# Expert slots that belong to one row tile of tokens, with scatter products on 64 partitions each

## What is computed

```python
def hier_moe(t, w_route_group, w_route_expert, w_gate_up, w_down):
    g_logits = jnp.einsum('td,dg->tg', t, w_route_group, ...)
    grp = jnp.argmax(g_logits, axis=-1)
    ...
    top_v, top_i = lax.top_k(e_prob, 2)
    ...
    for g in range(N_EXPERT_GROUPS):
        gu = jnp.einsum('td,edf->tef', t, w_gate_up[g])
        act = silu(gu[..., :512]) * gu[..., 512:] * combine[:, g, :, None]
        out = out + jnp.einsum('tef,efd->td', act, w_down[g])
    return out
```

## Time and profile before

| | us |
|---|---|
| median of 3 runs | 1650.46 (1649.89 to 1651.84) |
| the profiled execution | 1652.1 |
| its span | 1650.3 |
| TensorE busy in the span | 1601.2 (97%) |
| VectorE, ScalarE busy | 619.9, 449.0 |
| granted TensorE clock, mean | 0.994 |
| first expert layer's products | from 309 to 774 |
| second expert layer's products | from 1178 to 1642 |

### The profile page before, as it was taken

How to read it: one execution, slowest core, us unless ns; L and a number is a source line. 1 busy time by engine, 2 the same in 40 slices (tenths; PEclk the granted TensorE clock), 3 DMA queues, 4 the chain that set the end, 5 groups by cost and what they waited for, 6 DMA issues and landing times.

```text
span 1650.3 us, 21196 instructions
## 1 busy us (share of the span) xinstructions
PE 1601.2 (97%) x7929; PEld 934.2 (57%) x7929; DVE 619.9 (38%) x1356; ACT 449.0 (27%) x1168; POOL 142.2 (9%) x295
## 2 busy tenths in 40 slices
PE   9998879999999999999999999999999999999997
PEld 7877667653444344344877888877653444344342
DVE  4589993321322222123023544554421322222123
ACT  3488872211111111112143142232311111111112
POOL 1233341100000000001001202230000000000000
PEclk9999989999999999999999999999999999999999
DMA  9668777499999999999434956696599999999995
GB/s 340 204 212 264 219 237 286 151 400 401 427 428 424 429 428 424 430 425 399 175 132 162 331 183 239 173 275 285 226 401 402 429 426 425 429 427 426 430 424 214
DMA packets 107589, 542.24 MB, mean 329 GB/s; under 512 B 8780, under 2 KB 33556, under 8 KB 78546
## 3 DMA queue, kind: packets, MB, share of 16 engines
q1 hardware_dynamic: 90518, 485.20, 73.0%
q0 software_dynamic: 16672, 55.53, 10.7%
q10 hardware_dynamic: 316, 0.37, 0.1%
HBM read 524.81 MB, written 16.45 MB: 328 GB/s over the span
## 4 chain that ended last, share of the span: by engine, by line
PE 78%; DVE 10%; DMA 5%; ACT 4%; issue 2%; POOL 0%; SPq 0%; DVEq 0%; ACTq 0%
PE bank L1049 25%; PE bank L1413 14%; PE bank L1061 13%; PE bank L1032 5%; PE bank L1055 4%; PE bank L884 4%; DMA ring<-in_moe_w_gate_up 3%; PE bank L1344 3%; PE bank L1316 3%; DVE arena L2452 2%; PE bank L1642 2%; DVE arena L2297 2%; PE bank L1075 1%; ACT arena L1764 1%; DVE arena L2460 1%
## 5 line engine op out<-in xcount | busy, mean ns | idle before, releaser
L1049 PE MATMUL bank<-ring,arena 128*64 128x512 f32 x1520 | 335.7, 592 | 2.9 <-DMA ring<-in_moe_w_gate_up 2.8
L1413 PE MATMUL bank<-hT,ring 128*128 128x264 f32 x1152 | 269.4, 389 | 0.2
L1413 PEld LDWEIGHTS bank<-hT,ring 128*128 128x128 f32 x1152 | 214.4, 190 | 41.2 <-issue 3.9
L1049 PEld LDWEIGHTS bank<-ring,arena 128*64 128x64 f32 x1520 | 111.7, 137 | 214.4 <-issue 214.1
L2297 DVE TENSOR_TENSOR arena<-arena,bank 128x512 f32<-128x512 f32 x32 | 34.2, 1070 | 389.2 <-ACT arena L1764 389.2
L1061 PE MATMUL bank<-ring,arena 128*64 128x512 f32 x768 | 170.1, 595 | 1.6 <-DVE arena L2218 1.6
L1055 PE MATMUL bank<-arena 128*128 128x512 f32 x256 | 127.0, 618 | 1.6 <-ACT arena L1774 1.6
L1764 ACT ACTIVATE arena<-bank 128x512 f32<-128x512 f32 x32 | 19.1, 597 | 386.0 <-PE bank L1049 386.0
L2244 DVE SCALAR_TENSOR_TENSOR arena<-arena 128x1024 f32<-128x1024 f32 x32 | 41.1, 1284 | 213.2 <-ACT arena L1774 213.2
L1049 PE MATMUL bank<-arena 128*64 128x512 f32 x512 | 112.6, 592 | 0.0
L1061 PEld LDWEIGHTS bank<-ring,arena 128*64 128x64 f32 x768 | 53.8, 137 | 101.8 <-issue 99.7
(11 more groups left out here) (348 smaller groups left out, 1713.2 us busy)
## 6 DMA issues: line engine op xcount, KB each, us to landing
ring<-in_moe_w_gate_up SPq DMA_DIRECT2D x78, 2048.0 KB, 18.6
ring<-in_moe_w_down SPq DMA_DIRECT2D x48, 2048.0 KB, 23.6
arena<-in_moe_w_gate_up SPq DMA_DIRECT2D x32, 2048.0 KB, 18.9
ring<-in_attn_qkv SPq DMA_DIRECT2D x18, 2048.0 KB, 11.6
ring<-in_moe_w_gate_up SPq DMA_DIRECT2D x34, 1024.0 KB, 17.6
arena<-in_moe_w_down SPq DMA_DIRECT2D x32, 1024.0 KB, 21.2
ring<-in_ssm_in_proj SPq DMA_DIRECT2D x10, 2048.0 KB, 14.2
out<-arena POOLq DMA_DIRECT2D x24, 512.0 KB, 4.3
```

The source lines that it names most:

```text
L1049: mm = pe.matmul(bank[j][e * SLOTS:(e + 1) * SLOTS, :], Xg[:, 4 * half + k, 2 * (p % 2) + e, :], gate_rows(2 * half + e, p, k, first)[:, j ...
L1413: mm = pe.matmul(bank[i % 2][:, 0:T], wv[:, k, (i % 4) * P:(i % 4 + 1) * P], hT[:, k, :], start=(n == 0), stop=(n == DT - 1))
```

## The change

Slots now belong to a tile: each expert has 2 x 32 slots, 28 for prompt tokens of that tile and 4 for sample tokens (HALF = 32, FREE = 28, SAMP = 4; still 5 possible rounds). Ranks are counted per tile, so the product across tiles goes. A gather writes each tile's columns without adding up: 112 columns instead of 224. The gate, up and down products and the weight stream stay as they are. ScalarE copies the result rows in four pieces of 32 partitions per half, so that rows lie tile by tile (tile 0 on partitions 0 to 63, tile 1 on 64 to 127). A scatter then uses its tile's 64 partitions, and the first two scatters of a pair are of the two tiles, same half of the width. The shares are transposed by matmuls against the identity onto those partitions, and `CmT` is half as wide. Gathers 0 and 1 are moved up, ahead of the wait for the product. After the last pair the scatters go tile by tile.

```diff
-FREE = SLOTS - NS
-ROUNDS = -(-TP // FREE)
+TILES = TP // P
+SAMP = NS // TILES
+FREE = SLOTS // TILES - SAMP
+ROUNDS = -(-P // FREE)
+HALF = SLOTS // TILES
...
-                for t in range(2):
-                    for u in range(t + 1):
-                        mm = pe.matmul(bank[0][:, (t + 1) * NE:(t + 2) * NE], (strict if u == t else ones)[:, :], msk[:, u, :],
-                                       start=(u == 0), stop=(u == t))
-                mm.then_inc(m_rk, 1)
+                pe.matmul(bank[0][:, NE:3 * NE], strict[:, :], msk[:, 0:2, :].rearrange("p t e -> p (t e)"),
+                          start=True, stop=True).then_inc(m_rk, 1)
...
+                    out = bank[4 + i % 2][:, 0:16 * FREE].rearrange("p (d e t s) -> p d e t s", d=2, e=4, t=TILES)
                     for c in range(2):
                         d = 2 * i + c
-                        for t in range(2):
-                            mm = pe.matmul(bank[4 + i % 2][:, c * 4 * FREE:(c + 1) * 4 * FREE],
-                                           xn_e[:, t, d * P:(d + 1) * P],
-                                           Pm[:, t, :, :].rearrange("p e s -> p (e s)"),
-                                           start=(t == 0), stop=(t == 1))
+                        for t in range(TILES):
+                            mm = pe.matmul(out[:, c, :, t, :], xn_e[:, t, d * P:(d + 1) * P], Pm[:, t, :, :],
+                                           start=True, stop=True)
...
-                def scatter(j):
-                    pe.matmul(bank[6 + j % 2][:, :], CmT[:, (j // 2) * P:(j // 2 + 1) * P], ysl[:, j % 2, :],
-                              start=True, stop=True).then_inc(s.sc, 1)
+                def scatter(t, q, b):
+
+                    r = slice(t * SLOTS, (t + 1) * SLOTS)
+                    pe.matmul(bank[6 + b][:, :], CmT[r, :], ysl[r, q, :], start=True, stop=True).then_inc(s.sc, 1)
...
-                                scatter(j)
-
+                                scatter(j, 0, j)
+
+                        if h == 1 and not last:
+                            pe.wait_ge(s.peq, it * 2 + f + 2)
+                            for i in range(2):
+                                pe.wait_ge(s.xg, it * 8 + 4 * f + 3 + i)
+                                gather(i)
                         pe.wait_ge(s.act, it * 4 + p + 2)
...
-                                scatter(j)
+                                scatter(j - 2, 1, j - 2)
                         pe.wait_ge(s.cm, it * 4 + p + 1)
-                        for t in range(2):
-                            mm = transpose(bank[1][:, t * P:(t + 1) * P], Cm[:, h, t, :, :].rearrange("p e s -> p (e s)"))
+                        for t in range(TILES):
+                            mm = pe.matmul(bank[1][t * SLOTS:(t + 1) * SLOTS, 0:P], Cm[:, h, t, :, :].rearrange("p e s -> p (e s)"),
+                                           ident[:, :], start=True, stop=True)
                         mm.then_inc(s.tp, 1)
 
                         if h == 1 and not last:
-                            pe.wait_ge(s.peq, it * 2 + f + 2)
-                            for i in range(4):
+                            for i in range(2, 4):
...
                 for j in range(2):
-                    scatter(j)
+                    scatter(0, j, j)
...
-                    scatter(j)
+                    scatter(1, j - 2, j - 2)
...
+                def rows_by_tile(q):
+
+                    for e in range(2):
+                        for t in range(TILES):
+                            i, o = (TILES * e + t) * HALF, (2 * t + e) * HALF
+                            ins = act.activation(ysl[o:o + HALF, q, :], bank[2 + q][i:i + HALF, :], ACT.Copy)
+                    return ins
...
-                    act.activation(CmT[:, :], bank[1][:, 0:TP], ACT.Copy).then_inc(s.cpt, 1)
+                    act.activation(CmT[:, :], bank[1][:, 0:P], ACT.Copy).then_inc(s.cpt, 1)
...
-                    act.activation(ysl[:, 0, :], bank[2][:, :], ACT.Copy).then_inc(s.y, 1)
+                    rows_by_tile(0).then_inc(s.y, 1)
                     act.wait_ge(s.dn, it * 2 + 4)
-                    act.activation(ysl[:, 1, :], bank[3][:, :], ACT.Copy).then_inc(s.y, 1)
+                    rows_by_tile(1).then_inc(s.y, 1)
```

More of the change, by code:

```diff
@@ L225, in bass_hybrid_step @@
         cc = m(2, RC)
[L226 removed]
+        CmT = m(P)
         ysl = m(2, 512)
@@ L988, in moe @@
                     transpose(bank[7][:, d * NS:(d + 1) * NS], xn_e[0:NS, 2, d * P:(d + 1) * P])
-                for u in range(2):
-                    mm = pe.matmul(bank[7][:, 2 * P:2 * P + NE], ones[:, :], msk[:, u, :], start=(u == 0), stop=(u == 1))
-                mm.then_inc(m_rk, 1)
+                pe.matmul(bank[7][:, 2 * P:2 * P + 2 * NE], ones[:, :], msk[:, 0:2, :].rearrange("p t e -> p (t e)"),
+                          start=True, stop=True).then_inc(m_rk, 1)
                 def chunk_landed(j, it, p):
@@ L1070, in gather_pair @@
                 def gather_pair(i, e, b):
+                    out = bank[b][:, 0:8 * FREE].rearrange("p (d e t s) -> p d e t s", d=2, e=2, t=TILES)
                     for c in range(2):
                         d = 2 * i + c
-                        for t in range(2):
-                            mm = pe.matmul(bank[b][:, 2 * c * FREE:2 * (c + 1) * FREE],
-                                           xn_e[:, t, d * P:(d + 1) * P],
-                                           Pm[:, t, e:e + 2, :].rearrange("p e s -> p (e s)"),
-                                           start=(t == 0), stop=(t == 1))
+                        for t in range(TILES):
+                            mm = pe.matmul(out[:, c, :, t, :], xn_e[:, t, d * P:(d + 1) * P], Pm[:, t, e:e + 2, :],
+                                           start=True, stop=True)
                     return mm
@@ L2119, in expert_buffers @@
                 link(v.memset(wcol[:, :], 0.0))
-                link(v.tensor_copy(sel8[0:NS, :, :], ident[0:NS, 0:SLOTS].unsqueeze(1).to_broadcast([NS, 2, SLOTS])))
-                link(v.tensor_tensor(selT[:, :], ident[:, 0:NS], ident[:, SLOTS:SLOTS + NS], ALU.add))
+                link(v.memset(sel8[0:NS, :, :], 0.0))
+                link(v.tensor_copy(sel8[0:NS, :, :].rearrange("p t (e s) -> p t e s", e=2)[:, :, :, FREE:],
+                                   ident[0:NS, 0:NS].rearrange("p (t s) -> p t s", t=TILES).unsqueeze(2).to_broadcast(
+                                       [NS, TILES, 2, SAMP])))
+                rows = ident[:, :].rearrange("p (t e s) -> p t e s", e=2, t=TILES)[:, :, :, FREE:]
+                link(v.tensor_tensor(selT[:, :].rearrange("p (t s) -> p t s", t=TILES), rows[:, :, 0], rows[:, :, 1], ALU.add))
             def residual(l):
@@ L2279, in moe @@
                 spread = bank[7][:, P:P + NE].rearrange("p (q e) -> p q e", e=2)
-                for e in range(2):
-                    link(v.tensor_copy(wcol[e * SLOTS:(e + 1) * SLOTS, 1:1 + PAIRS], spread[e * SLOTS:(e + 1) * SLOTS, :, e]))
+                for i in range(2 * TILES):
+                    r = slice(i * HALF, (i + 1) * HALF)
+                    link(v.tensor_copy(wcol[r, 1:1 + PAIRS], spread[r, :, i % 2]))
                 v.sem_inc(s.acc, 5)
@@ L2318, in moe @@
                 v.wait_ge(s.acc, more * (4 * PAIRS) + 4 * PAIRS + 1)
-                add(last, s_xa, range(2))
+                add(last, s_xa, range(2), True)
                 for q in range(2):
@@ L2327, in moe @@
                     variance(4, 0, P)
-                add(last, s_xa, range(2, 4))
+                add(last, s_xa, range(2, 4), True)
             norm(0, gmix(0))
```

41 lines of the change are left out of this document (23 added, 18 removed).

## The result

The changed kernel is **slower**, by 0.66%: 1662.42 us median of 6 runs (1660.37 to 1668.59) beside 1651.15 for the kernel before, 6 runs (1649.70 to 1656.64). The ratio is 1.0066, 95% interval 1.0054 to 1.0079. Forecast were 1646.9 and at most 1654. The profiled execution took 1665.87 us, its span is 1664.2, 13.9 longer than before's 1650.3.

What follows compares the result with a forecast made beforehand. The weights' arrival was taken as the floor, with TensorE 0 to 1.4 us above it. Layers at -3.05 + 1.55 and -3.7 + 1.55 gave about -3.6: 1646.9 us from 1650.46, 8 in 10 range 1644 to 1654.

Steps and rivals of the forecast that it cites:

- rival (a): Expert loops: TensorE sets the pace after all, so its savings come through whole, 1610 us; chance 4%.
- A couple of scatters: Expert loop: two scatters on 64 partitions run side by side, 1.06 us instead of 1.92 (bounds 0.86 and 1.92).
- two pairs in 54.46 us: Expert loop: TensorE would need about 54.4 us for two pairs, 4.5 less than their weights.
- 1.5 us of waiting for the eviction: Pairs with gathers: gathers 2 and 3 wait for banks VectorE empties, some 1.6 us of TensorE waiting.
- the distance from the last landing: Second layer's last pair: TensorE gives up its lag behind the last weights' landing, gaining 1.05 us.
- The gap behind pair 1: Weight stream at each layer's start: pair 1 frees buffers 2.4 us earlier, closing gaps of 2.35 and 1.93 us.
- The early gathers themselves go from 112 to 56 columns: Each layer's start: weight loads hold the early gathers, so halving columns gains nothing (bounds 0 and 1 us a layer).
- Rival (c): TensorE's waits for weights drop the clock to 1.2 GHz, each fall costing 2 us; 1655 us, chance 13%.
- Loss 1.55 per layer: Each layer's tail: eight ScalarE copies 0.47 us apart delay the last scatters by 1.55 us (bounds 1.4 and 3).
- let TensorE wait 2.4 us before the last scatters: Each layer's tail: TensorE waits 2.4 us for the copies, where it had waited 0.80.
- the 6.75 us that the forecast had ahead of the tails: Both layers before their tails: earlier weights and shorter ends gain 3.05 us in the first, 3.7 in the second.
- the 3.6 forecast for the change: Whole kernel: gains before the tails less both tail losses, about 3.6 us off the median of 1650.46.

Runs made afterwards that it cites:

- the filler: Changed kernel with 15 products nobody reads put ahead of the last scatters' wait for the copies; 1662.17 us, ratio 1.0048.
- Repaired singly: Changed kernel with all four experts gathered early at once, second set dropped (1656.42 us, 1.0021), or with down products in 32-column tiles, one copy per half (1655.04 us, 1.0016).
- quarters and wide: Changed kernel with down products in 32-column tiles and early gathers streaming 112 columns, half of them kept, second set staying; 1649.14 us, ratio 0.9978.
- The repaired kernel: Changed kernel with down products in 32-column tiles and all four experts gathered early at once, second set dropped; 1645.79 us, ratio 0.9964.

## Why the prediction was wrong

The forecast was 1646.9 us and at most 1654; measured were 1662.42.

What held, by its own steps. The weights are what the middle of a layer waits for: 427 GB/s before and after, so rival (a) is out. A couple of scatters in 1.06 us (forecast 1.06), gathers 0.12 each, two pairs in 54.46 us (54.4), 1.5 us of waiting for the eviction, 24.5 us of waiting for weights. On the scatters the Trainium skill, "TensorEngine Tiling (Array Packing)", section Theoretical Speedup, gives up to 2x for a contraction of 64 or less. The trace has 1.91 / 1.06 = 1.8, and in the loop it turned into waits for weights. Of the steps by which it was to reach the end, the distance from the last landing in the second layer was given up as forecast: TensorE starts the last pair 0.14 us behind the landing, at 1619.98. The gap behind pair 1 closed in the second layer (406 to 434 GB/s in every 4 us from 1240 to 1256) but not in the first, where the clock fell under pair 1's own gathers (3.55 us for the 16 at 366.77, for 2.04 in the second layer) and the stream still shows 291 GB/s from 376 to 380. That loses about 1.3 us of the 2.35 that the gap cost.

What failed:

**1. "The early gathers themselves go from 112 to 56 columns ... I give them no gain (bounds 0 and 1 us a layer)."** This is the step that failed: a loss wasn't among the bounds, and the early gathers with the first gate half behind them cost 7.7 us more in the two layers. Their duration at full clock was forecast rightly (3.72 for the second set), but what the narrow products do to the clock was put at nothing. Rival (c) had the clock and its evidence, the 0.73 from 310 to 315 us. It priced a fall at each layer's early products at 2 us, from a fall of 4 us that no row shows, had a chance of 13%, and stayed outside the sum. Measured are 3.27 and 4.40 us more at the two starts. Inside the layers, where (c) expected two falls in every two pairs, the profile has five falls in all, some 3.4 us each, and 24.5 us of waits, and the clock is 0.98 from 500 to 700 us. Shown from both sides: wider gathers in the changed kernel -6 us, thinner ones in the kernel before +5 us. What starts the fall is open: it can come before the first early gather, behind a wait of 1.35 us and short router products that the kernel before has too. The single rank product and VectorE's longer list don't start it alone, since the kernel with wide gathers has both and no fall at either start.

**2. "Its time goes by columns ... so 0.47 apart ... Loss 1.55 per layer (bounds 1.4 and 3)."** The mechanism held and the size was off. The copies stand 0.60 apart. The way from the last gate and up products to the last scatters grew by 2.2 and 2.5, inside the bounds; the term was undersized by 0.7 to 0.9 a layer. The row chosen was of other copies: three to the residual rows, each from a bank of its own. The nearer row was the copy itself at 0.60, named at the start of the same paragraph. The Trainium skill, "VectorE: DVE Perf Modes", section The TRN2 errata, prices ScalarE's copy out of PSUM at 172 cycles and one per column, of 1.2 GHz, from which I estimate 0.57 us for 512 columns. The trace agrees within 5%: 0.589 with 32 partitions and 0.597 with 128.

**3. The tail's own second price.** The working let TensorE wait 2.4 us before the last scatters and charged only the wait; the clock behind it was put at nothing. TensorE waited 3.32 us, the clock fell just behind the wait in both layers, and the scatters, the samples' products and the norm cost 1.8 + 0.4 us in the first layer (the 0.4 is VectorE's transposed rows, 5.01 for 4.60; every kernel of the new layout has it, at full clock too, and its cause was not looked for) and 1.65 in the second. All 12 tails with this wait (six profiles) show a fall in the wait or within 2 us behind it, and none of the 16 others does, the filler's among them; so the fall is the wait's. The four copies in the kernel before show 7.3 us for wait and clock together. The Trainium skill, "TensorE: Matmul & The Clock Gate", section HAM oscillation, puts such falls down to a matmul loop's waits for data. The tail agrees. The layer starts neither confirm nor refute it: a wait of 1.35 us stands ahead of every second layer's start, with a fall behind it and without, and under the thin gathers the clock stays down while TensorE is busy throughout.

The two parts add up. Repaired singly they leave ratios of 1.0021 and 1.0016; repaired together 0.9964, faster than the kernel before by 7.8 us of the medians and 6.0 by the ratio. The figure to hold against this is the 6.75 us that the forecast had ahead of the tails, since the repair takes the copies' loss away too; that quarters and wide gains 3.6 us by its ratio (0.9978), the 3.6 forecast for the change, is chance. The repaired kernel also drops the second set of early gathers, and quarters and wide keeps it. The 0.0014 between the two may be that set's share, but the intervals overlap, and the clock fell at the layers' starts in one profile and not in the other. In the old layout the dropped set gave no gain (1.0018).

## What to carry to other kernels

When a change makes TensorE's products narrower, or lets it wait, ahead of long products, price the clock over the products behind them and not only the instructions themselves; the place to ask is where a stage begins and ends, since inside a loop that waits for weights a slower product costs little. When an engine's one instruction becomes four, look first at where no other work covers it, and take the distance from that same copy's row, not from a neighbour's. And where transfers are the floor, count the waits for them before and after: they are the reserve. Here it was 24.5 us, and for the 24.0 us of work beyond it the kernel got 17 us longer.

## What was not expected of the hardware

TensorE can be busy for all of 20 us and be granted half its clock for two thirds of them (thin early gathers in the kernel before: PE busy 20.00, clock 0.66). The clock had fallen 1.6 us before the 56-column products, each with its own 128 x 128 weights, and stayed down under all of them; twice the columns in as many instructions took 3.83 us in the profile of wide early gathers, at clock 1.00, where the thin ones took 6.9. Four tiles of 32 columns run at the price of two of 64 (7.07 us each way). Four ScalarE copies of 32 partitions out of one bank stand 0.60 us apart, while three copies out of three banks stand 0.47 apart; why is open. The falls are chance in part: with 112-column early gathers they came at 6 of 14 layer starts, and the kernel with quarters and wide gathers spread over 9 us in 12 runs, of which one was profiled.
